# The second chunk's state multiply of a chunked scan reads PSUM, and the first chunk's copy follows it

## Reference, cut to what matters

```python
states = jnp.einsum('bcsgn,bcgrs,bcsgrp->bcgrpn', Bc, decay_states, xdt)
chunk_decay = jnp.exp(a_cs[..., -1])

def step(carry, inp):
    st, dec = inp
    return carry * dec[..., None, None] + st, carry

init = jnp.zeros((b, G, r, P, N), jnp.float32)
_, prev = lax.scan(step, init, (jnp.moveaxis(states, 1, 0), jnp.moveaxis(chunk_decay, 1, 0)))
y_off = jnp.einsum('bclgn,bcgrpn,bcgrl->bclgrp', Cc, prev, jnp.exp(a_cs))
...
y_fwd = ssd_chunked(xs, dt[:, :, 0], A[0], Bm, Cm)
y_bwd = fl(ssd_chunked(fl(xs), fl(dt[:, :, 1]), A[1], fl(Bm), fl(Cm)))
```

## Time and profile before

| | |
|---|---|
| median of 3 runs | 2535.12 us (2534.81 to 3506.26) |
| profiled execution, its own time | 2533.52 us |
| its span, first to last instruction | 2531.7 us |
| PE busy | 2466.2 us (97%) |
| DVE busy | 1466.1 us (58%) |
| ACT busy | 1168.2 us (46%) |
| POOL busy | 162.2 us (6%) |
| chain that ended last | PE 79%, DVE 11%, ACT 6%, issue 3% |

### The profile page before, as it was taken

One profiled execution on the slowest core, in us unless ns is written; L12 is line 12 of the kernel. 1 busy time (PEld: TensorE's weight loads), 2 busy tenths in 40 slices (PEclk: granted clock), 3 DMA queues, 4 the chain that ended last, 5 costly groups with the idle time before them and its releaser, 6 DMA issues.

```text
span 2531.7 us, 35862 instructions
## 1 busy us (share of the span) xinstructions
PE 2466.2 (97%) x14408; PEld 2008.6 (79%) x14408; DVE 1466.1 (58%) x2366; ACT 1168.2 (46%) x2091; POOL 162.2 (6%) x156
## 2 busy tenths in 40 slices
PE   9999999999999999999999899999999999999998
PEld 6888778888777678888877788887877877888886
DVE  6665554433656564344378898786676556543343
ACT  5354353322456644233257676666455444432232
POOL 2110110000100010000001111111000010100001
PEclk9999999999999999999999999999999999999999
DMA  5222234534322223333324333333322233233322
GB/s 155 76 60 76 59 102 112 131 104 119 95 87 82 67 70 106 92 100 92 99 62 132 100 117 101 109 116 112 110 67 67 96 121 100 78 106 100 95 97 75
DMA packets 201781, 243.42 MB, mean 96 GB/s; under 512 B 8080, under 2 KB 133296, under 8 KB 201360
## 3 DMA queue, kind: packets, MB, share of 16 engines
q1 hardware_dynamic: 201616, 241.12, 32.0%
HBM read 231.00 MB, written 9.57 MB: 95 GB/s over the span
## 4 chain that ended last, share of the span: by engine, by line
PE 79%; DVE 11%; ACT 6%; issue 3%; DMA 1%; POOL 0%; DVEq 0%; SPq 0%; ACTq 0%; POOLq 0%
PE bank L1978 22%; PE bank L1980 22%; PE bank L1979 22%; DVE CV L2687 2%; DVE wlo L2462 2%; PE bank L1984 1%; PE bank L1985 1%; PE bank L1986 1%; PE bank L1997 1%; ACT E L2387 1%; ACT whi L2247 1%; PE bank L2179 1%; PE bank L2187 1%; PE bank L2200 1%; DVE h L2496 1%
## 5 line engine op out<-in xcount | busy, mean ns | idle before, releaser
L2462 DVE TENSOR_TENSOR wlo<-raw,whi 128x1024 fp32r<-128x1024 f32 x389 | 491.2, 1269 | 627.8 <-ACT whi L2247 625.5
L2247 ACT ACTIVATE whi<-raw 128x1024 fp32r<-128x1024 f32 x389 | 406.9, 1053 | 580.3 <-PE bank L1980 568.2
L1978 PE MATMUL bank<-XAh,whi 128*128 128x512 f32 x1552 | 615.4, 397 | 6.4 <-DVE XAl L2470 3.4
L1980 PE MATMUL bank<-XAh,wlo 128*128 128x512 f32 x1552 | 601.6, 388 | 0.0
L1979 PE MATMUL bank<-XAl,whi 128*128 128x512 f32 x1552 | 601.5, 388 | 0.0
L1978 PEld LDWEIGHTS bank<-XAh,whi 128*128 128x128 f32 x1552 | 291.6, 188 | 78.8 <-issue 12.1
L1980 PEld LDWEIGHTS bank<-XAh,wlo 128*128 128x128 f32 x1552 | 291.5, 188 | 61.1
L1979 PEld LDWEIGHTS bank<-XAl,whi 128*128 128x128 f32 x1552 | 291.8, 188 | 57.5 <-issue 1.0
L1978 PE MATMUL bank<-XBh,whi 128*128 128x512 f32 (+1 forms) x840 | 331.7, 395 | 1.8 <-DVE XBl L2468 1.6
L1980 PE MATMUL bank<-XBh,wlo 128*128 128x512 f32 (+1 forms) x840 | 324.0, 386 | 0.0
L1979 PE MATMUL bank<-XBl,whi 128*128 128x512 f32 (+1 forms) x840 | 323.7, 385 | 0.0
(11 more groups left out here) (330 smaller groups left out, 3255.5 us busy)
## 6 DMA issues: line engine op xcount, KB each, us to landing
raw<-in_w_in SPq DMA_DIRECT2D x77, 512.0 KB, 4.1
raw<-in_up SPq DMA_DIRECT2D x64, 512.0 KB, 3.7
raw<-in_down SPq DMA_DIRECT2D x64, 512.0 KB, 3.8
raw<-in_a_w_in SPq DMA_DIRECT2D x32, 512.0 KB, 4.2
E<-scr_rows SPq DMA_DIRECT2D x32, 512.0 KB, 5.6
raw<-in_w_up SPq DMA_DIRECT2D x32, 512.0 KB, 3.6
raw<-in_w_down SPq DMA_DIRECT2D x32, 512.0 KB, 3.6
raw<-in_w_kv SPq DMA_DIRECT2D x16, 512.0 KB, 3.6
```

Of the source, the lines that this page charges most:

```text
L1978: pe.matmul(out, wh[:, w, c], xh[:, x, r], start=st, stop=False)
L1980: m = pe.matmul(out, wl[:, w, c], xh[:, x, r], start=False, stop=en)
L2247: act.activation(s.hi, s.raw, ACT.Copy).then_inc(s.whi[0], 1)
L2462: dve.tensor_tensor(s.lo, s.raw, s.hi.bitcast(F32), ALU.subtract).then_inc(s.wlo[0], 1)
```

## The change

The first multiply of a pass reads the first chunk's state in PSUM in place of ACT's copy of it. DVE no longer waits for ACT: it waits for the states (and for the room in PH) itself. ACT's copy into slot 0 waits for the new signal `read`, which DVE gives with the first add, and which also takes the place of DVE's own link. The copy is then needed by PE's carry products alone, so `sc_carry` waits for `first` and `passed`. `banks[0]` is free after `first`, `banks[1]` after `passed`. The number of instructions with data is the same on every engine.

```diff
-                s5 = add("sc_pass", dr=dr, banks=bs, PH=PH, et=et, g=g, states=s4.states, ph_free=ready.get(("PH", dr), NONE), first=sig("sc.first"), passed=sig("sc.passed"))
-                for b in bs:
-                    b.free(s5.passed)
-                passed.append(s5.passed)
+                s5 = add("sc_pass", dr=dr, banks=bs, PH=PH, et=et, g=g, states=s4.states, ph_free=ready.get(("PH", dr), NONE), read=sig("sc.read"), first=sig("sc.first"), passed=sig("sc.passed"))
+                bs[0].free(s5.first)
+                bs[1].free(s5.passed)
+                passed.append([s5.first, s5.passed])
...
         elif k == "sc_carry":
-            on.wait_ge(*s.passed)
+            for v in s.passed:
+                on.wait_ge(*v)
...
         elif k == "sc_pass":
-            on.wait_ge(*s.states)
+            on.wait_ge(*s.read)
             on.wait_ge(*s.ph_free)
             act.activation(s.PH[:, s.dr, 0, :], s.banks[0].t[:, 0:256], ACT.Copy).then_inc(s.first[0], 1)
...
-            on.wait_ge(*s.first)
+            on.wait_ge(*s.states)
+            on.wait_ge(*s.ph_free)
             for n, c in ((1, 1), (2, 2)) if s.dr == 0 else ((1, 2), (2, 1)):
-                dst, pv = s.PH[:, s.dr, n, :], s.PH[:, s.dr, n - 1, :]
+                dst, pv = s.PH[:, s.dr, n, :], s.banks[0].t[:, 0:256] if n == 1 else s.PH[:, s.dr, 1, :]
                 dve.tensor_tensor(r4(dst), r4(pv), s.et[:, c, e0:e0 + 4].unsqueeze(2).to_broadcast([P, 4, 64]), ALU.mult).then_inc(*on.link())
                 on.linked()
                 m = dve.tensor_tensor(dst, dst, s.banks[n // 2].t[:, n % 2 * 256:n % 2 * 256 + 256], ALU.add)
                 if n == 1:
-                    m.then_inc(*on.link())
-                    on.linked()
+                    m.then_inc(s.read[0], 1)
+                    on.wait_ge(*s.read)
             m.then_inc(s.passed[0], 1)
```

## The result

The changed kernel takes 2540.91 us (median of 10 runs, 2540.05 to 2962.25), the kernel before 2534.97 us in the runs beside it: +5.94 us, a ratio of 1.0024 with a 95% interval of 1.0016 to 1.0033. The forecast was 2541, from a sum of +6.1 us. A second measurement on another chip gave 2541.32 against 2534.91 us, +6.4 us (1.0025, 1.0016 to 1.0035).

A forecast was written before the change was run, and what follows sets the result against it. It took DVE and ACT to bound groups 0 to 3 of the scan and PE the rest; 2.6 + 2.4 + 0.5 + 0.6 = 6.1 us took the median from 2535.1 to 2541.2, point 2541, range 2532 to 2547.

The forecast's parts named there:

- The bound: Scan stage: delays in groups 0 to 3 (passes 1 to 8) reach the end one for one; later ones meet slack.
- the chain's return to PE: The step at 1549.61, where the chain that ended last goes back to PE, would come about 6 us later.
- With few steps on PE: Up to about 1549 us the chain that ended last runs over DVE and ACT, seldom PE.
- Added: the wait: ACT's copy waits for DVE's first add: 2.6, 2.4, 0.5 and 0.6 us in passes 1, 2, 3 and 5.
- The other two terms: Pass 3: DVE's wlo waits 0.5 us for whi; pass 5: DVE's taps wait 0.6 us for a late convolution start.
- ACT idle time: ACT would stand in front of the copy in some 12 of 16 passes, 40 us or so in all.
- Passes 9 to 16: 0 us: Groups 4 to 7: ACT's waits for PE and three slots of units cover the delay; 4 us without cover.
- Removed: DVE's wait: Pass 4's 5.24 us wait for ACT's copy: 0 us gained, up to -5.2 us if the cover weren't there.
- Changed: the source: 16 of 32 multiplies read PSUM instead of SBUF: 0 us, at 415 to 425 ns each.
- A: Rival: the 6.1 us are absorbed in the mixed chain before 1549, leaving 0 to +2 us, about 2535; chance 0.25.
- B: Rival: faster, about 2530 us, as pass 4's removed wait wins 5.2 us; chance 0.12.
- C: Rival: the coupling goes on after 1470, 0.5 us in each of passes 6 to 16, about 2547; chance 0.13.

The follow-up runs named there:

- e8: The change in pass 1 alone (group 0, direction 0), against the kernel before: 2537.76 against 2534.93 us, +2.83.
- e6: The kernel before with only ACT's wait for DVE's first add put in, behind its copy: 2540.44 against 2534.79 us, +5.65.
- e1: The whole change measured again on another chip, with its profile, against the kernel before: 2541.32 against 2534.91 us, +6.41.
- e3: The change in passes 3 to 8 alone (groups 1 to 3), against the kernel before: 2534.72 against 2534.91 us, -0.19.
- e12: The change in pass 4 alone (group 1, direction 1), against the kernel before: 2534.49 against 2535.22 us, -0.73.
- e2: The change in passes 1 and 2 alone (group 0), against the kernel before: 2540.17 against 2534.91 us, +5.26.
- e9: The change in pass 2 alone (group 0, direction 1), against the kernel before: 2538.14 against 2534.93 us, +3.21.
- e4: The change in passes 9 to 16 alone (groups 4 to 7), against the kernel before: 2535.88 against 2534.91 us, +0.97.
- e10: The whole change with ACT's copy waiting for the pass's second add, against the kernel before: 2559.09 against 2534.93 us, +24.2.
- e5: The kernel before with only the first multiply's source changed to PSUM: 2534.17 against 2534.79 us, -0.62.
- e7: The whole change with ACT's copy moved to the carry step, against the kernel before: 2600.69 against 2534.79 us, +65.9.

## Why the prediction was right, and where it wasn't

**The bound.** Right for groups 0 to 3. What is done there goes to the end by way of DVE and ACT; e8's step of 2.59 us at pass 2 is its 2.83 us at the end. For the groups behind them, see below: the chain's return to PE comes at 1580.96, not 6 us behind 1549.61. "With few steps on PE" holds, 16 of the 214 us from 1335 to 1549; nearly all of them lie behind 1495.

**Added: the wait.** Right in kind (e6) and, for passes 1 and 2, in size: 2.58 and 2.43 us in e1's trace against 2.6 and 2.4. The other two terms, 0.5 and 0.6 us, are not borne out. In pass 3 DVE does wait the 0.48 us for whi, but nothing of it is left at pass 5: e3, with passes 3 and 4 changed, gains 0.16 us from pass 3 to pass 5, and e12, with pass 4 alone, 0.18. (In e1 the shift falls there, from 4.97 to 4.62 us; what gives it back wasn't separated.) Behind pass 5 e1 steps by 0.63 us against 0.6, and DVE waits the 0.48 us for whi there, but e2, e9 and e12, which leave pass 5 alone, step by 0.71, 0.67 and 0.43 at the same place: in e9 and e12 DVE waits 0.56 and 0.33 us for a convolution start that stood for PE. So that match is no proof of the term. Pass 6 was put at zero and has 1.4 us in e1, 0.1 back in e3. ACT idle time was forecast at 12 passes and 40 us, and is 15 and 61.7 us. That the copy had been done "long before" DVE in all passes but the fourth is right for most and not for pass 16, where it ended 0.05 us before DVE started; nothing hangs on it.

**Passes 9 to 16: 0 us.** This term was too small by a little: by the traces of e1 and e4, some 0.4 us per group, 1.5 to 1.7 us in all. The step had two supports. "Three slots of units cover" the odd ones: not around pass 10, where the unit's whi ended 0.1 us before PE took it, already in the trace of before. And "the next ACT instruction waited for PE until 1571.83 anyway" left 0.1 us of slack, reckoned with DVE's add at its old time; but the odd pass in front makes DVE 0.5 us late, which moves that add as well. Each pass was looked at alone. The median of e4 can't tell this from zero; the chain and PE's 0.60 us wait in e1, and e10, which adds to the hold and gets 3.3 us per group, show that the slack is used up.

**Removed: DVE's wait.** The price of 0 was right (e12), the cover was misnamed: not the tanh of 1433.83 in front of L2540, but ACT's whi behind it (with PE's carry before it in e12). The trace showed only that L2540 began when the pass ended, which says nothing on what it needed.

**Changed: the source.** Right: 417 ns, where 415 to 425 was forecast, and e5 shows no difference.

**The rivals.** Full absorption (A, up to +2 us) is refuted by e1 and e2, the gain of 5.2 us (B) by e12. Of C, the coupling going on with 5.5 us over passes 6 to 16, e1's trace has 3.1 us (5.25 to 8.34), some 1.5 of it in groups 4 to 7; e3 and e4 together have 1.5.

The 5.0 us of passes 1 and 2 were foreseen step by step. That the median fits to some 0.1 us is luck: the last 1.1 us of the sum were put at passes 3 and 5, while e2 alone has +5.26, and what the whole has beyond it comes in the traces from pass 6 and groups 4 to 7, which were put at zero. The two measurements of the whole, +5.94 and +6.41, differ by more than the fit.

## What to carry to other kernels

When a wait is turned round, ask which of the two engines used to come first: here ACT had been done with the copy 4 to 5 us ahead in the two passes that cost most, and that lead was what kept its queue in front of DVE. The engine that gets the new wait pays with everything queued behind it, and a busy share of 46% is no protection when the other engine needs the next item in that queue. Before taking a delay as covered, find the next instruction that PE needs from that queue and when it needs it, with the delays of the passes before it included; and moving the step further down an in-order list only helps until its reader, further ahead in the same list, becomes the one that waits (e7: +66 us for a 0.37 us copy).

## What the runs showed of the hardware

- A DVE multiply of 128x256 float32 with a broadcast factor takes 417 ns from PSUM (e1, e5) and 424 from SBUF, both medians.
- The second multiply of direction 1, beside POOL's L2853, takes up to 1558 ns where the first multiply reads SBUF and up to 1446 ns where it reads PSUM (e5; 1444 in e1). In both the multiply from SBUF that runs beside POOL's instruction is the slow one; the multiply from PSUM was never over 425 ns, but it started ahead of POOL's. The first add lies wholly beside POOL's instruction and isn't slowed: in pass 10 of before POOL works from 1569.66 to 1571.68, the add, with one input in PSUM, takes 0.42 us from 1569.95, and the multiply with both inputs in SBUF takes 1.56 us from 1570.40, to 0.28 us behind POOL's end.
- PE's granted clock fell where PE stood for the copies: in e7 it reads 0.94 in 1335 to 1510 us and 0.95 in 1510 to 1740 us, against 0.99 and 1.00 before, and the same 14408 instructions kept PE busy for 2482.9 us in place of 2466.2.
